# The low part of h made by GpSimd instead of VectorE, in a fused decoder layer on one core

## The reference

```python
def swiglu(h, w_gate, w_up, w_down):
    return (jax.nn.silu(h @ w_gate) * (h @ w_up)) @ w_down

x = x + 0.5 * swiglu(rmsnorm(x, norm_ffn1[l]), w1_gate[l], w1_up[l], w1_down[l])
...
x = x + jnp.concatenate([attn, pooled], axis=-1) @ w_out[l]
x = x + 0.5 * swiglu(rmsnorm(x, norm_ffn2[l]), w2_gate[l], w2_up[l], w2_down[l])
return rmsnorm(x, norm_final)
```

## Time and profile before

| what | value |
|---|---|
| median of 3 runs | 1687.75 us (1687.64 to 1688.31) |
| the profiled execution, its own time | 1687.65 us |
| its span in the profile | 1685.8 us |
| PE busy | 1674.9 us, 99% |
| DVE busy | 1457.2 us, 86% |
| ACT busy | 921.7 us, 55% |
| POOL busy | 233.6 us, 14% |
| share of the chain that ended last | PE 98%, DVE 1% |

### The profile page before, as it was taken

The page is one execution under the profiler, slowest core; times in us unless marked ns, Lnnn a source line. Parts: engine busy times, 40 slices in busy tenths (PEclk is TensorE's granted clock), DMA queues, the critical chain, the costliest instruction groups (busy, mean ns, idle before and its releaser), DMA issues.

```text
span 1685.8 us, 21945 instructions
## 1 busy us (share of the span) xinstructions
PE 1674.9 (99%) x7500; PEld 1389.3 (82%) x7500; DVE 1457.2 (86%) x1753; ACT 921.7 (55%) x1094; POOL 233.6 (14%) x397
## 2 busy tenths in 40 slices
PE   9999999999999999999999999999999999999998
PEld 7788888888888888888888888888888888888886
DVE  7999999999988787587977889999999999888896
ACT  6655555555555544454555545555555555555554
POOL 0222222222220000000040002222222222200000
PEclk9999999999999999999999999999999999999999
DMA  7677777777775655666544575777777777765564
GB/s 277 205 230 232 230 225 224 224 224 225 223 266 195 250 199 196 208 202 199 175 149 153 189 256 169 226 230 224 229 227 232 215 244 225 249 237 190 184 200 174
DMA packets 189502, 362.96 MB, mean 215 GB/s; under 512 B 12233, under 2 KB 24449, under 8 KB 189057
## 3 DMA queue, kind: packets, MB, share of 16 engines
q1 hardware_dynamic: 170528, 336.70, 59.3%
q0 software_dynamic: 16976, 24.14, 6.5%
q10 hardware_dynamic: 1936, 1.32, 0.3%
HBM read 346.39 MB, written 4.19 MB: 208 GB/s over the span
## 4 chain that ended last, share of the span: by engine, by line
PE 98%; DVE 1%; ACT 0%; issue 0%; DMA 0%; SPq 0%; ACTq 0%; DVEq 0%
PE banks L636 23%; PE banks L634 23%; PE banks L635 23%; PE banks L727 7%; PE banks L728 7%; PE banks L729 7%; PE banks L620 2%; PE banks L653 1%; PE banks L623 1%; PE banks L874 0%; PE banks L898 0%; DMA raw<-in_w_gate 0%; PE banks L886 0%; DVE w_lo L1373 0%; ACT gu L1051 0%
## 5 line engine op out<-in xcount | busy, mean ns | idle before, releaser
L1149 ACT ACTIVATE w_hi<-raw 128x1024 fp32r<-128x1024 f32 (+1 forms) x440 | 425.4, 997 | 288.9 <-PE banks L636 185.1
L1597 DVE TENSOR_TENSOR w_lo<-raw,w_hi 128x1024 fp32r<-128x1024 f32 (+1 forms) x440 | 491.4, 1144 | 52.6 <-ACT w_hi L1149 52.6
L634 PE MATMUL banks<-w_hi,act 128*128 128x512 f32 x1056 | 411.6, 390 | 0.0
L636 PE MATMUL banks<-w_lo,act 128*128 128x512 f32 x1056 | 410.9, 389 | 0.0
L635 PE MATMUL banks<-w_hi,act 128*128 128x512 f32 x1056 | 410.8, 389 | 0.0
L1187 ACT ACTIVATE w_hi<-raw 128x1024 fp32r<-128x1024 f32 x212 | 214.5, 1022 | 216.8 <-PE banks L636 170.9
L1692 DVE TENSOR_TENSOR w_lo<-raw,w_hi 128x1024 fp32r<-128x1024 f32 x212 | 246.5, 1177 | 75.6 <-ACT w_hi L1187 72.8
L634 PE MATMUL banks<-w_hi,h 128*128 128x512 f32 x688 | 267.8, 389 | 0.0
L636 PE MATMUL banks<-w_lo,h 128*128 128x512 f32 x688 | 267.7, 389 | 0.0
L635 PE MATMUL banks<-w_hi,h 128*128 128x512 f32 x688 | 267.6, 389 | 0.0
L2122 POOL DMA_DIRECT2D turned<-squared x320 | 170.9, 557 | 681.5 <-DVE squared L1448 675.7
(11 more groups left out here) (201 smaller groups left out, 1741.0 us busy)
## 6 DMA issues: line engine op xcount, KB each, us to landing
raw<-in_w_down SPq DMA_DIRECT2D x88, 1024.0 KB, 6.2
raw<-in_w_gate SPq DMA_DIRECT2D x84, 1024.0 KB, 5.2
raw<-in_w_up SPq DMA_DIRECT2D x84, 1024.0 KB, 5.4
raw<-in_w_in SPq DMA_DIRECT2D x32, 1024.0 KB, 5.4
raw<-in_w_out SPq DMA_DIRECT2D x16, 1024.0 KB, 5.0
turned<-squared POOLq DMA_DIRECT2D x320, 32.0 KB, 1.8
raw<-in_w_up POOLq DMA_DIRECT2D x20, 512.0 KB, 7.0
raw<-in_w_up SPq DMA_DIRECT2D x8, 512.0 KB, 9.4
```

The lines of the kernel that those rows point to most:

```text
L634: pe.matmul(dst, operand[:, k, hi], w_hi[:, s, w], start=k == first, stop=False)
L636: mm = pe.matmul(dst, operand[:, k, hi], w_lo[:, s, w], start=False, stop=k == last)
L1149: act_e.activation(fast_split(w_hi, p, shift), fast_raw(name, shift), ACT.Copy).then_inc(hi_ready, 1)
L1597: dve.tensor_tensor(fast_split(w_lo, p, shift), fast_raw(ORDER[p], shift), fast_split(w_hi, p, shift).bitcast(F32), ALU.subtract).then_inc ...
```

## The change

In the ten superblocks of the loop, in both nets, the subtraction that makes the low part of h leaves VectorE and is made by GpSimd, behind its accumulating transfer. GpSimd waits there for the high part (`h_hi_ready`) and for the count of its own earlier subtractions. Before each `exchange` GpSimd waits for `h_ready` too, since `turned` is written anew. The count `h_ready` now has two writers, so ACT and DVE wait in `down` for GpSimd's last one before they treat the last superblock's h, which stays with VectorE.

```diff
@@ ScalarE, down
                     if p == ROW_LAST_H_AT:
+                        act_e.wait_ge(h_ready, sb - 1)
                         round_h(sb - 1, FT - SB, last_turned)
@@ VectorE, fast_gate_up
                     elif name == "U14":
                         fold_v_n5_n7()
-                        split_h(fi - 1, SB * i - SB, turned)
@@ VectorE, down
                     if p == ROW_LAST_H_AT + 1:
+                        dve.wait_ge(h_ready, sb - 1)
                         split_h(sb - 1, FT - SB, last_turned)
@@ GpSimd
+            def split_h(n, k):
+
+                pool.wait_ge(h_hi_ready, n + 1)
+                pool.wait_ge(h_ready, n)
+                by_square = "p k (m j) -> p k m j"
+                pool.tensor_tensor(h[:, k:k + SB, S:2 * S].rearrange(by_square, j=SQ),
+                                   turned[:, :, :, :].rearrange("p m k j -> p k m j"),
+                                   h[:, k:k + SB, 0:S].rearrange(by_square, j=SQ).bitcast(F32),
+                                   ALU.subtract).then_inc(h_ready, 1)
+
                 for i in range(1, GATE_SBS):
+                    pool.wait_ge(h_ready, f["sb"] + i - 1)
                     exchange(f["sb"] + i - 1, turned)
                     slot = raw_slot("u0", 0 if i % 2 else 2)
                     pool.wait_ge(summed, len(SUMS) * (f["fast"] + i - 1) + SUMS.index("t1") + 1)
...
                                    accum_op=ALU.add).then_inc(t3_landed, 16)
+                    split_h(f["sb"] + i - 1, SB * (i - 1))
```

## The result

| | median of 3 | profiled execution | span |
|---|---|---|---|
| before | 1687.75 us | 1687.65 us | 1685.8 us |
| with the change | 1708.69 us (1708.08 to 1709.68) | | 1706.6 us |

A forecast was written before the change was run, and what follows sets the result against it. The prediction took TensorE as the bound, losing time only where it waits: 20 waits of 0.93 us at U10 add 18.6 us to 1687.65, giving 1706.2 us; range 1691 to 1730.

The forecast's parts named there:

- What bounds the kernel: Whole kernel: TensorE, busy for 99% of the span, is the bound; time changes only where it waits.
- What is removed: End of each superblock: taking twenty subtractions of 1.22 us each off VectorE is worth 0.
- When GpSimd runs: Around T3: GpSimd can start at about 126.1, gets in at about 126.6; the fold is not held, U10's split is.
- How long it holds: GpSimd's subtraction beside U10's split: 2.41 us, scaled from L2113; other rows gave 1.89 and 4.51 us.
- The sum: At U10: split 1.68 us late, less 0.75 us of lead, leaves a 0.93 us TensorE wait, 20 times: 18.6 us.
- Leads behind U10: Pieces after U10: leads shrink by 0.75 us and no more; U12 keeps about 1.6 us, F0 0.7.
- No change: Rival at U10: its split is late by less than 0.75 us, so the time stays 1687.7; chance 0.12.
- A long hold: Rival at GpSimd's subtraction: short inner runs of 32 elements make it as costly as L2112, 1748 us; blocked for longer, 0.09.
- A gain: Rival at the superblock's end: VectorE's saved 1.14 us counts 20 times, 23 us, giving 1665; chance 0.03.
- The two rules: Skill guidance on GpSimd's subtraction: blocking VectorE to the record's end gives 1709; an estimated 2.25 us operation gives 1703.

The follow-up runs named there:

- the run with two tiles: Against the changed kernel, GpSimd makes two of the four h tiles and VectorE the other two behind U14; 1688.63 us, ratio 1.0005.

## Why the prediction was right

**What bounds the kernel.** TensorE, and only its waits count: borne out. The extra time is 20 waits at U10 and what follows each of them; all else is as long as before to 0.3 us.

**What is removed: 0.** The run with both subtractions shows it (1708.81 against 1708.69, where the runs of one kernel lie within 2 us).

**When GpSimd runs.** Forecast: asks 0.5 us before T3's split ends (it was 0.6), gets in at its end, the fold with a PSUM input is not held, U10's split is. All four stand in the rows above. That GpSimd gets in even against a split that touches the one before was not needed for the sum, and was shown by the run with the fold moved away.

**How long it holds.** Taken from L2113 by size: 2.41 us. The operation alone takes 2.40. The record beside a split is 2.88 us since it begins 0.6 us early; behind T3's split it is 2.27. That what GpSimd needs before it first reads passes while it waits would explain the 0.13 us less; no run separates it. The term was 0.14 us too large, and 0.06 of that was made good by T3's end, which the sum put at 126.6 and not at 126.66. The rows with twice the time for half the elements (L2112) did not apply: about 1 us of each was waiting, as the prediction had thought possible.

**The sum.** U10's split late by 2.84 - 1.22 = 1.62 us, forecast 1.68. TensorE's wait 0.88, forecast 0.93. To it come 0.11 us for the first matmul behind a wait and some hundredths in those that follow, which the prediction did not have: 0.99 and more against 0.93. Twenty times 0.99 is 19.8 of the 20.8 us of the span. One superblock of the twenty waited 1.33 us instead of 0.88: ScalarE's L1085 started there at 1368.24, behind the start of T3's split at 1367.83 and not before it, and GpSimd got in 0.45 us later than elsewhere. The hundredths make 0.3 us, and 0.3 lie outside the loops' waits. The prediction said 1706, the measurement 1708.69: the hold was a little too large in the sum, the price of a wait too small, and that the two errors have opposite signs is luck. The missing term could have been read in the trace of before: the matmul at 55.62 is 0.50 us long and not 0.39.

**Leads behind U10** shrank and none ran out, as said; F0 kept 0.9 us (its split ends at 139.94, its first matmul starts at 140.86), forecast 0.7; VectorE idled for 2.35 us before F0's split, forecast 2.4.

**The rivals.** No change needed a hold of at most 1.48 us: the run with two tiles (1.14 us) and the one in four parts are that case. A long hold did not come about: GpSimd alone took 2.40 us, so the short runs of 32 elements did not make it slow. A gain did not either: VectorE idled before F0, and the run with both subtractions was no slower than the change.

**The two rules.** By the Trainium skill, "SBUF — State Buffer", section "Who interferes with whom", as the prediction took it, VectorE would stand to the end of GpSimd's instruction, 1709; U10's split went on 0.13 us before that. The time came out at 1708.69 for another reason, the slower first matmul. By the estimate of 2.25 us from the Trainium skill, "GPSIMD Engine Reference", section "Elementwise — side-by-side cycle accounting", it would have been 1703; GpSimd alone took 2.40.

## What to carry to other kernels

An operation moved from VectorE to GpSimd is not taken off VectorE if both read SBUF with two inputs: GpSimd's version stops VectorE for nearly its own, longer, time (here 2.27 us less 0.13), and at the place where it falls. Before such a move, set VectorE's and TensorE's timelines side by side and read, piece by piece, how far ahead VectorE is: the cost is what the hold makes VectorE late less that lead, and 0.11 us for each wait, times the number of places; below the lead it is nothing. If the lead is too short, start the operation in a stretch where VectorE idles, or cut it in parts so that the two engines take turns; here both brought the time back to that of before.

## What the runs showed of the hardware that was not expected

- GpSimd's memsets, 2.97 us of writing to SBUF, cost VectorE's two-input splits nothing at all.
- GpSimd's record for 1024 elements ends 0.9 us behind T3's split with one input and 2.27 with two: more than twice as long.
- The multiplication of L2112 (one input, 512 elements) ends 1.36 us behind the VectorE operation that it waited for, and lets VectorE go 1.04 us before its own end.
- The first matmul behind a wait for w_lo costs 0.11 us beyond the wait wherever such a wait was found in the loops, be it 0.12 or 1.33 us long.
- A waiting GpSimd instruction gets in between two VectorE splits that stand back to back, so a VectorE that is never idle does not keep GpSimd out.
